# Fewer lookup batches beside a merge, half-size gate buffers, 2 KB key rows and an early half of the output weights

## The reference

```
z = rmsnorm(x); columns of z @ w_in: retention q,k,v; attention q,k,v; gate logits ga, gb
r_out = rms_norm(retention(...))                 # 4 heads, decay per head, chunks of 128
a_out = rms_norm((A1 - lam*A2) V)                # 4 heads, two maps of 64, causal
m = sigmoid(ga) * (r_out @ w_br_ret) + sigmoid(gb) * (a_out @ w_br_att)
h = x + m @ w_out
z2 = rms_norm(h)
per token, 8 heads: top 16 of 128x128 experts by the sum of two half scores, softmax gates
act = gelu(u[ids] . z2) * gate;  h += sum(act * v[ids])   # u, v: 16384 rows of 1024
y = rms_norm(h)
```

## Time and profile before

| what | us |
|---|---|
| median of three runs | 4201.55 (4199.16 to 4207.85) |
| the profiled execution | 4203.96 |
| its span | 4202.1 |
| PE busy | 3194.1 (76%) |
| DVE busy | 2589.5 (62%) |
| POOL busy | 1294.6 (31%) |
| ACT busy | 670.5 (16%) |
| moved by DMA | 1002.69 MB, mean 239 GB/s |

### The profile page before, as it was taken

One profiled execution on the slowest core, in us unless ns is written; L12 is line 12 of the kernel. 1 busy time (PEld: TensorE's weight loads), 2 busy tenths in 40 slices (PEclk: granted clock), 3 DMA queues, 4 the chain that ended last, 5 costly groups with the idle time before them and its releaser, 6 DMA issues. The chain is left out here.

```text
span 4202.1 us, 32255 instructions
## 1 busy us (share of the span) xinstructions
PE 3194.1 (76%) x10192; PEld 1860.9 (44%) x10192; DVE 2589.5 (62%) x5283; ACT 670.5 (16%) x1711; POOL 1294.6 (31%) x930
## 2 busy tenths in 40 slices
PE   6998988998884644754465333698999899999995
PEld 3553435774562412322233333355555555555553
DVE  2221134001598864689569877487778778787876
ACT  1110012001112401122110333011111111111111
POOL 0000000000133232366323555244444444444442
PEclk9999975999995666877787666799999999999997
DMA  4002000112213597799741366899999999999996
GB/s 133 0 1 71 25 11 35 53 53 108 68 36 138 188 339 255 319 416 418 283 164 30 124 254 252 333 413 384 388 401 416 384 403 400 395 407 409 405 376 254
DMA packets 265660, 1002.69 MB, mean 239 GB/s; under 512 B 26306, under 2 KB 117458, under 8 KB 180242
## 3 DMA queue, kind: packets, MB, share of 16 engines
q0 software_dynamic: 95728, 687.91, 40.4%
q1 hardware_dynamic: 164370, 304.30, 20.1%
q10 hardware_dynamic: 5392, 8.42, 0.5%
HBM read 952.70 MB, written 47.85 MB: 238 GB/s over the span
## 5 line engine op out<-in xcount | busy, mean ns | idle before, releaser
L198 POOL DMA_INDIRECT lk_rows<-in_expert_uv,lk_ids x640 | 1031.6, 1612 | 1369.3 <-DVE lk_sums L239 1269.6
L239 DVE SCALAR_TENSOR_TENSOR lk_sums<-lk_rows,lk_weights,lk_sums 128x1024 f32<-128x1024 f32 x647 | 829.8, 1283 | 38.6 <-DVE lk_sums L239 1.4
L1963 PE MATMUL ps<-zT_B,ex_u 128*128 128x384 f32 x2048 | 716.0, 511 | 171.5 <-DMA ex_u<-in_expert_uT 171.5
L208 DVE SCALAR_TENSOR_TENSOR lk_rows<-lk_rows,lk_z_rows 128x1024 f32<-128x1024 f32 x648 | 772.6, 1223 | 62.3 <-DMA lk_rows<-in_expert_uv,lk_ids 57.6
L1976 PE MATMUL ps<-ex_a,ex_v 128*128 128x384 f32 x2048 | 672.4, 489 | 27.5 <-DVE accT L2011 16.5
L1963 PEld LDWEIGHTS ps<-zT_B,ex_u 128*128 128x128 f32 x2048 | 407.3, 200 | 474.8 <-DMA ex_u<-in_expert_uT 191.4
L1976 PEld LDWEIGHTS ps<-ex_a,ex_v 128*128 128x128 f32 x2048 | 389.7, 191 | 305.1 <-DVE accT L2011 26.3
L216 ACT ACTIVATE lk_weights<-lk_weights 128x2 f32<-128x2 f32 x324 | 66.0, 204 | 1792.8 <-DVE lk_rows L208 1792.6
L1560 POOL MEMSET rtA_scores<- 128x128 f32 x2 | 0.4, 204 | 1014.5 <-POOLq L86 1014.5
L2011 DVE TENSOR_TENSOR accT<-accT,ps 128x384 f32<-128x384 f32 x248 | 128.3, 548 | 268.7 <-PE ps L1976 268.7
L1871 PE MATMUL ps<-ga_onehot_i,ga_onehot_j 128*128 128x128 f32 x768 | 104.6, 299 | 145.4 <-issue 94.9
(11 more groups left out here) (379 smaller groups left out, 3647.8 us busy)
## 6 DMA issues: line engine op xcount, KB each, us to landing
ex_u<-in_expert_uT SPq DMA_DIRECT2D x128, 512.0 KB, 14.3
ex_v<-in_expert_v SPq DMA_DIRECT2D x128, 512.0 KB, 11.6
gate_scratch<-ga_stage SPq DMA_DIRECT2D x3, 8192.0 KB, 68.0
ex_gates<-gate_scratch SPq DMA_DIRECT2D x128, 192.0 KB, 8.5
mgA_w<-in_w_merge SPq DMA_DIRECT2D x8, 1792.0 KB, 7.4
mgB_w<-in_w_merge SPq DMA_DIRECT2D x8, 1792.0 KB, 11.0
lk_rows<-in_expert_uv,lk_ids POOLq DMA_INDIRECT x640, 10.9
w_ret<-in_w_ret SPq DMA_DIRECT2D x4, 2048.0 KB, 18.4
```

What stands on the lines that cost most here:

```text
L198: pool.indirect_dma_start(out=self.slot[:, s, :], out_offset=None, in_=self.a["expert_uv"], in_offset=bass.IndirectOffsetOnAxis(ap=index, ...
L208: self.nc.vector.scalar_tensor_tensor(out=u, in0=u, scalar=1.0, in1=self.z[:, t % 2, :], op0=ALU.mult, op1=ALU.mult, accum_out=self.w[:, t ...
L239: self.nc.vector.scalar_tensor_tensor(out=total, in0=v, scalar=w, in1=total, op0=ALU.mult, op1=ALU.add).then_inc(self.added, 1)
L1963: last = nc.tensor.matmul(ps[:, n % HB, 0:DENSE], U[:, n % UB, k, :], zD[:, k, :], start=(k == 0), stop=(k == KD - 1))
```

## The change

Four edits and what carries them:

- `merge_phase` of half B does 3 lookup batches per step instead of 7 (half A has no lookup). Over eight steps that is 24 batches instead of 56.
- `gate_phase` keeps and stores 64 tokens at a time in two buffers of the same total size, and does 2 batches after each of the six parts instead of 8 after each of three tiles. The stored rows are 256 B instead of 512 B. ScalarE waits only for the store before the last one.
- The key pages are laid out dimension, head, token on the host, so that a partition's four heads lie together in a row of 2 KB. The on-chip layout is the same.
- A scope `OutWeights` around merge and residual holds the two halves of the output weights. The first is loaded at the end of merge's SP queue, the second at the start of residual. Its semaphores are cleared at the scope's end, with one more barrier.

What a stage no longer looks up is left to `expert_phase`, which gets 324 - 76 = 248 batches.

```diff
-        merge_phase(nc, a, ps, mem, B, MERGE_B, look)
-        residual_phase(nc, a, ps, ident, mem, B, RES_B, h_dram, z_dram, look)
+        with OutWeights(nc, a, mem, B, MERGE_B, RES_B) as w_out:
+            merge_phase(nc, a, ps, mem, B, MERGE_B, w_out, look)
+            residual_phase(nc, a, ps, ident, mem, B, RES_B, w_out, h_dram, z_dram, look)
...
-                                 a["cache_kT"][ds(page(b, pg), 1)].rearrange("o h p n -> p (o h) n")
+                                 a["cache_kT"][ds(page(b, pg), 1)].rearrange("o p h n -> p (o h) n")
...
+class OutWeights(Scope):
+    def __init__(self, nc, a, mem, half, merge, res):
+        super().__init__(nc)
+        self.a = a
+        self.cols = [mem.place(f"w_out{half.name}{b}", [P, KD, BANK], res if b else merge, res) for b in range(2)]
+        self.loaded = [self.queue_sem(f"w_out_loaded{half.name}{b}") for b in range(2)]
+        self.callback(self.zero)
+    def load(self, sp, b):
+        sp.dma_start(self.cols[b][:, :, :], self.a["w_out"][:, :, b * BANK:(b + 1) * BANK]).then_inc(self.loaded[b], 16)
...
-        PER = -(-7 // nb)
+        PER = 3 if nb == 1 else 2
...
                 sp.dma_start(w[:, k % 2, :, :], a["w_merge"][k]).then_inc(w_in[k % 2], 16)
+            w_out.load(sp, 0)
...
-            for b in range(2):
-                cols = slice(b * BANK, (b + 1) * BANK)
-                sp.dma_start(w[:, :, cols], a["w_out"][:, :, cols]).then_inc(w_in[b], 16)
+            w_out.load(sp, 1)
             sp.dma_start(gain[:, :], a["g_ffn"].partition_broadcast(P)).then_inc(s_gain, 16)
...
-        PER = P // GT
+        HT = P // 2
+        PER = HT // GT
         SETS = 3
-        BETWEEN = 8
+        BETWEEN = 2
-        stage = sb("stage", [P, NK, P])
+        stage = sb("stage", [P, 2, NK, HT])
-        out = sem("stored")
-        steps = range(DT * PER)
+        out = [sem(f"stored{u}") for u in range(2)]
+        steps = range(2 * DT * PER)
...
-                if tile and local == 0:
-                    act.wait_ge(out, ONE + 16 * tile)
+                if part >= 2 and local == 0:
+                    act.wait_ge(out[part % 2], ONE + 16 * (part // 2))
...
-            for t in range(DT):
-                sp.wait_ge(kept, ONE + PER * (t + 1))
-                sp.dma_start(g_dram[:, :, t * P:(t + 1) * P].rearrange("i j t -> j i t"),
-                             stage[:, :, :]).then_inc(out, 16)
+            for n in range(2 * DT):
+                sp.wait_ge(kept, ONE + PER * (n + 1))
+                sp.dma_start(g_dram[:, :, n * HT:(n + 1) * HT].rearrange("i j t -> j i t"),
+                             stage[:, n % 2, :, :]).then_inc(out[n % 2], 16)
...
-        "cache_kT": c(np.asarray(i["cache_k"])[0].transpose(0, 2, 3, 1)),
+        "cache_kT": c(np.asarray(i["cache_k"])[0].transpose(0, 3, 2, 1)),
```

More of the change, by code:

```diff
@@ L320, in build @@
         attention_phase(nc, a, ps, ident, mem, A, ATT_A, KT, VA, lam, None)
-        merge_phase(nc, a, ps, mem, A, MERGE_A, None)
-        residual_phase(nc, a, ps, ident, mem, A, RES_A, h_dram, z_dram, None)
+        with OutWeights(nc, a, mem, A, MERGE_A, RES_A) as w_out:
+            merge_phase(nc, a, ps, mem, A, MERGE_A, w_out, None)
+            residual_phase(nc, a, ps, ident, mem, A, RES_A, w_out, h_dram, z_dram, None)
         routing_phase(nc, a, ps, ident, mem, A, ROUTE_A, look, None, gs_dram, is_dram)
@@ L1261, in _, with merge_phase @@
                                     gain[:, 0:1], 1.0 - LAM_INIT, ALU.mult, ALU.mult).then_inc(a_kept, 1)
-def merge_phase(nc, a, ps, mem, half, stage, look):
+class OutWeights(Scope):
[7 more added lines that the diff above has]
+        sp.dma_start(self.cols[b][:, :, :], self.a["w_out"][:, :, b * BANK:(b + 1) * BANK]).then_inc(self.loaded[b], 16)
+def merge_phase(nc, a, ps, mem, half, stage, w_out, look):
     NW = 2 * KD + KD + AH
@@ L1335, in _, with residual_phase @@
                                         ALU.add).then_inc(merged, 1)
-def residual_phase(nc, a, ps, ident, mem, half, stage, h_dram, z_dram, look):
+def residual_phase(nc, a, ps, ident, mem, half, stage, w_out, h_dram, z_dram, look):
     with Scope(nc) as ctx:
@@ L1345, in sems @@
             return [ctx.sem(f"rs{half.name}_{n}{u}") for u in range(2)]
-        gain, w = sb("gain_ffn", [P, D]), sb("w_out", [P, KD, D])
+        gain = sb("gain_ffn", [P, D])
         x, h, z = sb("x", [P, 2, D]), sb("h", [P, 2, D]), sb("z", [P, 2, D])
@@ L1351, in residual_phase @@
         s_gain = ctx.sem(f"rs{half.name}_gain_ffn_loaded")
-        w_in = sems("w_out_loaded")
         x_in, ready, added, out, squared, mean, root, inverse, scaled, z_out, turned, kept = (sems(n) for n in (
@@ L1419, in product @@
                 for b in range(2):
-                    pe.wait_ge(w_in[b], ONE + 16)
+                    pe.wait_ge(w_out.loaded[b], 16)
                     for c in range(KD):
-                        last = nc.tensor.matmul(ps[0:rows, 2 * u + b, :], m[:, c, :], w[:, c, b * BANK:(b + 1) * BANK],
+                        last = nc.tensor.matmul(ps[0:rows, 2 * u + b, :], m[:, c, :], w_out.cols[b][:, c, :],
                                                 start=(c == 0), stop=(c == KD - 1))
@@ L1877, in _ @@
             for n in steps:
-                s, tile, local = n % SETS, n // PER, n % PER * GT
+                s, part, local = n % SETS, n // PER, n % PER * GT
                 act.wait_ge(done, ONE + n + 1)
-                if tile and local == 0:
-                    act.wait_ge(out, ONE + 16 * tile)
-                nc.scalar.activation(stage[:, :, local:local + GT].rearrange("p i t -> p t i"),
+                if part >= 2 and local == 0:
+                    act.wait_ge(out[part % 2], ONE + 16 * (part // 2))
+                nc.scalar.activation(stage[:, part % 2, :, local:local + GT].rearrange("p i t -> p t i"),
                                      ps[:, 2 * s:2 * s + 2, :].rearrange("p b (t i) -> p (b t) i", i=NK),
@@ L1889, in _ @@
         def _(sp):
-            for t in range(DT):
-                sp.wait_ge(kept, ONE + PER * (t + 1))
-                sp.dma_start(g_dram[:, :, t * P:(t + 1) * P].rearrange("i j t -> j i t"),
-                             stage[:, :, :]).then_inc(out, 16)
-            sp.wait_ge(out, ONE + 16 * DT)
+            for n in range(2 * DT):
+                sp.wait_ge(kept, ONE + PER * (n + 1))
+                sp.dma_start(g_dram[:, :, n * HT:(n + 1) * HT].rearrange("i j t -> j i t"),
+                             stage[:, n % 2, :, :]).then_inc(out[n % 2], 16)
+            for u in range(2):
+                sp.wait_ge(out[u], ONE + 16 * DT)
 def expert_phase(nc, a, ps, mem, half, g_dram, accT, look):
```

## The result

The changed kernel takes 4092.5 us (median; 4088.4 to 4098.1) against 4204.7 us beside it: ratio 0.9735, 95% interval 0.9718 to 0.9753. The forecast was 4118 us; the kernel is faster by 112 us where the forecast's sum had 85.

A forecast was written before the change was run, and what follows sets the result against it. It took the second merge and expert stage as DMA-bound, the gate stage as alternating between waiting for a store and having none. -158 - 16 - 5 - 111 + 205 = -85 from 4203.96 us, stated as 4118 us; range 4070 to 4195.

The forecast's parts named there:

- Second merge: Merge stage of half B: with 24 batches instead of 56 the next stage starts earlier, -158 us, between -150 and -165.
- Output weights: Both residual stages: with the first half loaded early, TensorE starts without waiting; -8 us twice, -4 to -9 each.
- Key pages: Sample stage: larger key rows shorten the wait for keys in seven samples; -5 us, 0 to -15.
- Gate stage: Gate stage: 30 us per 64-token part, 18 us per store; -111 us, or -80 at 25 us per store.
- rival of the dear store: Gate stage: 256 B rows cost more than 512 B rows, 50 us per store; kernel slower, 4299 us; chance 0.13.
- three cycles per packet: Gate stores: about 3 cycles over a packet's 32 B beats, so 316 GB/s and an estimated 13 us per store.
- Pricing the store by rows alone: Gate stage rival: a store still takes 25 us at equal row count; gate -80, total 4149 us; chance 0.22.
- Expert stage: Expert stage: the added batches make a step 13.2 us and the stage 1716 us; +205 us, between +180 and +237.
- in steady state it runs at 398 GB/s and share 0.99: Expert stage before the change: taken as bound by the DMA engines, with TensorE close behind.
- the expert stage has room: Expert stage rival: TensorE sets the pace, DMA only near its limit; +116 instead of +205, 4030 us; chance 0.08.

## Why the prediction was right, and where it was off

The stages' sum of -85 us gives 4116.6 us by the prediction's own steps (4204.0 - 85 - 2.4); the 4118 is a slip of 1 us. What follows goes by the stages.

**Second merge, right,** 6 us short. TensorE's last product ends 156.3 us after the start, where 156 were said, and its warm steps take the 18.4 us of before. DMA was said to come out beside it, and it does: share 1.01 at 418 GB/s. The miss is what the sum gave no price, the two together: VectorE waits 12.7 us for gathered rows, starts its last lookup 144.4 us after the stage's start instead of 141.4 and takes 16.5 us for it instead of 15. So the last gather is issued at 162 us instead of 156, and the tail of 15 us follows.

**Output weights, right** within 1 us for the residual stages, by the run without the large edits too; there the early load lengthened the merge of half B by 6 us, about the 5 us of its bytes, as the merge was still full. In the changed kernel it is not hidden either: the merge takes 177 us with it and took 173 without it (the run with the merge edit alone). Merge A, whose queue was idle, pays nothing (257 us before and after).

**Key pages, right in sign,** larger than said (8 for 5), inside its bounds. TensorE waits less for the pages; that the higher rate of longer rows does it, as the forecast had it, is not shown.

**Gate stage, right** to 2 us (each store lands in 29.1 to 31.0 us, where under 30 was said), and for the stated reason: the part's pace is 30.0 us, VectorE's, and 18 us per store was near: 28.7 us from the last issue to its landing, less 10 us for its two batches, are 18.7, and 4.19 MB at 268 GB/s are 15.7. The rival of the dear store is out: no doubling shows at 256 B. It stood on the rule of the Trainium skill ("DMA: Bandwidth & Descriptors", section Specifications) of a read-modify-write below 512 B; whether the chip does that no run shows, but as a price it is not in these traces. By the same page's three cycles per packet (section Why small descriptors are slow), 316 GB/s were estimated and 268 measured. Pricing the store by rows alone, 25 us, was wrong from 512 to 256 B and would be nearly right from 256 to 128 B.

**Expert stage, mis-sized:** +171 for +205. These 34 us are the whole error of the forecast and more than it (the span fell by 115.6 us where the sum had 85); the merge's 6 and the gates' 2 us hide a part. The failing step is "in steady state it runs at 398 GB/s and share 0.99", read as a full queue from which 13.2 us a step followed. Measured are 12.9 us a step, (1682 - 26) / 128, at 414 GB/s. Two things show it: deeper buffers alone gave 413 GB/s at the old load, and the rate rose with each load (399, 406, 412, 414). Steps have one batch or two. One with two needs 5.44 MB, 13.1 us at 414 GB/s; one with one leaves the DMA engines time while TensorE works 10.8 us; three buffers evened this out only in part, as the dips at 3096 and 3140 us show. Before, 76 of 128 steps had two; now 120 have. So the first batches moved filled gaps. The rival "the expert stage has room" had the right direction and came true with 34 of its 89 us. It had in its favour a row I listed and passed over: VectorE waited only 25.6 us for gathered rows.

**Where the gain comes from.** Merge alone -39, gates alone -66, keys and weights -22: -127, and together -112. The 15 us between are, to 1 us, the bent curve: the expert stage pays +115 and +40 for the two moves apart and +171 for both.

## What to carry to other kernels

Moving work between two stages bound by the same resource gains only what that stage has unused, so ask which stage is truly full. A busy share of 0.99 over a long stretch is not the proof: cut the stretch into windows of a few microseconds and look for dips, compare the rate with the best that a full stretch reaches (here 418 in the merge), and see whether the consumers of the transfers ever wait. Where the load per step alternates, deeper buffers and more load fill the same gaps, and the gain of one is not there for the other. A fixed wait at a stage's end may be hiding transfers that the next stage's start would otherwise meet.

## What the runs showed of the hardware that was not expected

- Stores to HBM in rows of 512, 256 and 128 B: 333, 268 and 145 GB/s over sixteen engines. The cost of a row fell from 512 to 256 B, where a doubling had been feared.
- With stores of 16384 rows of 128 B, each 36.0 us on its way, the issue of one held SP for 17.8 us in the median.
- The mix of 8 KB gathers, weights and gates sustains 414 GB/s for 1570 us; the forecast had 410 from 418 for gathers and 385 for the rest.
- With the merge's TensorE running through, its granted clock in the stage was 0.92 against 0.74; in the fuller expert stage, where TensorE waits more, it fell from 0.96 to 0.92. TensorE was busy for 1433 us there instead of 1378 with the same products, while the stage ran at the DMA engines' 414 GB/s.
